# Block one of a two-block transformer: another order of turning, attention and rounding, and the cumulated gates spread by transfer

## The reference

```python
h = _layernorm(x, ln_in_g, ln_in_b)
for layer in range(DEPTH):                      # 2 layers
    proj = jnp.einsum('bsd,de->bse', h, w_in[layer])
    (aq, ak, av, ag, bq, bk, bv, bf, bg, cq, ck, cv, cg) = jnp.split(proj, SPLIT_POINTS, axis=-1)
    # A: 4 heads of differential attention: softmax(q1 k1) - lam * softmax(q2 k2), rotary q and k
    oa = _differential_attention(qa[:, :, 0], qa[:, :, 1], ka[:, :, 0], ka[:, :, 1], va, lam)
    ya = _from_blocks(rms(oa) * subln_g[layer] * (1.0 - lam_init)) * jax.nn.silu(ag)
    # B: 4 heads, softmax(s + cum[q] - cum[k]), cum the cumulated log gates
    logf = jax.nn.log_sigmoid((bf + b_forget[layer]).astype(jnp.float32))
    cum_logf = jnp.cumsum(logf, axis=1).transpose(0, 2, 1)
    ob = _forgetting_attention(_split_heads(bq, HB), _split_heads(bk, HB), _split_heads(bv, HB), cum_logf)
    yb = _from_blocks(ob) * jax.nn.silu(bg)
    # C: 4 heads of stick-breaking attention, z = q k * scale
    #   weights = exp(log_sigmoid(z) + reverse_cumsum(log_sigmoid(-z)) without its own term)
    oc = _stick_breaking_attention(_split_heads(cq, HC), _split_heads(ck, HC), _split_heads(cv, HC))
    yc = _from_blocks(oc) * jax.nn.silu(cg)
    y = jnp.einsum('bse,ed->bsd', jnp.concatenate([ya, yb, yc], axis=-1), w_out[layer])
    h = _layernorm(DEEPNORM_ALPHA * h + y, ln_g[layer], ln_b[layer])
```

## Time and profile before

| | us |
|---|---|
| median of 3 runs | 1867.9 (1865.4 to 1868.3) |
| the profiled execution | 1866.4 |
| its span, first to last instruction | 1864.6 |
| PE busy | 1730.1 |
| block one, by the step list | 0 to about 850 |

### The profile page before, as it was taken

How to read it: one execution, slowest core, us unless ns; L and a number is a source line. 1 busy time by engine, 2 the same in 40 slices (tenths; PEclk the granted TensorE clock), 3 DMA queues, 4 the chain that set the end, 5 groups by cost and what they waited for, 6 DMA issues and landing times. The chain is left out here.

```text
span 1864.6 us, 21015 instructions
## 1 busy us (share of the span) xinstructions
PE 1730.1 (93%) x7750; PEld 1311.8 (70%) x7750; DVE 864.3 (46%) x1487; ACT 799.2 (43%) x1512; POOL 594.1 (32%) x291
## 2 busy tenths in 40 slices
PE   7999999889999998989998999998999899999997
PEld 4766766578667665677564777777787788888786
DVE  5543335553533345454598548475556222221402
ACT  3334446533344455344323555565643334443411
POOL 2613212135313121144120332333265424444440
PEclk9998999899989998999999999999999989999999
DMA  6412222014222120114121222322274333333221
GB/s 177 108 34 68 57 57 68 12 61 112 57 57 57 53 83 23 46 46 130 34 65 51 73 80 68 125 74 68 89 240 135 90 89 93 102 91 102 90 79 45
DMA packets 203832, 148.81 MB, mean 80 GB/s; under 512 B 14926, under 2 KB 183506, under 8 KB 203732
## 3 DMA queue, kind: packets, MB, share of 16 engines
q1 hardware_dynamic: 199056, 132.45, 24.9%
q0 software_dynamic: 4528, 14.95, 2.4%
q10 hardware_dynamic: 148, 0.07, 0.0%
HBM read 136.96 MB, written 10.49 MB: 79 GB/s over the span
## 5 line engine op out<-in xcount | busy, mean ns | idle before, releaser
L1435 POOL TENSOR_TENSOR weights_rounded<-weights_raw,weights_rounded 128x1024 fp32r<-128x1024 f32 (+1 forms) x237 | 566.7, 2406 | 1146.8 <-ACT weights_rounded L1973 1146.7
L1506 PE MATMUL proj<-hT_high,weights_rounded 128*128 128x512 f32 (+1 forms) x1904 | 640.2, 408 | 17.5 <-POOL weights_rounded L1435 7.5
L1506 PEld LDWEIGHTS proj<-hT_high,weights_rounded 128*128 128x128 f32 x1904 | 369.7, 195 | 108.4 <-issue 23.7
L1506 PE MATMUL proj<-hT_low,weights_rounded 128*128 128x512 f32 (+1 forms) x952 | 378.9, 398 | 0.0
L1973 ACT ACTIVATE weights_rounded<-weights_raw 128x1024 fp32r<-128x1024 f32 (+1 forms) x237 | 234.0, 1008 | 112.4 <-DMA weights_raw<-in_w_ffn_down 59.0
L1502 PE MATMUL proj<-weights_rounded,hT_high 128*128 128x512 f32 (+1 forms) x640 | 203.9, 395 | 22.2 <-DVE branches_low L2456 13.5
L1506 PEld LDWEIGHTS proj<-hT_low,weights_rounded 128*128 128x128 f32 x952 | 186.0, 195 | 38.8 <-issue 3.7
L1502 PEld LDWEIGHTS proj<-weights_rounded,hT_high 128*128 128x128 f32 x640 | 122.3, 195 | 50.9 <-issue 15.7
L1629 PE MATMUL score<-qk 64*128 64x256 f32 (+3 forms) x256 | 81.0, 501 | 18.6 <-ACT E L1835 10.2
L1672 PE MATMUL attn_out<-probs_T,V 128*64 128x128 f32 (+1 forms) x560 | 89.2, 294 | 0.0
L1658 PE MATMUL turned_probs<-constants,probs 128*128 128x128 f32 x320 | 61.8, 295 | 18.5 <-ACT probs_T L1863 18.2
(11 more groups left out here) (473 smaller groups left out, 2779.8 us busy)
## 6 DMA issues: line engine op xcount, KB each, us to landing
weights_raw<-in_w_in SPq DMA_DIRECT2D x113, 512.0 KB, 4.0
weights_raw<-in_w_out SPq DMA_DIRECT2D x24, 512.0 KB, 3.8
weights_raw<-in_w_ffn_gate SPq DMA_DIRECT2D x22, 512.0 KB, 3.9
weights_raw<-in_w_ffn_up SPq DMA_DIRECT2D x22, 512.0 KB, 3.8
weights_raw<-in_w_ffn_down SPq DMA_DIRECT2D x22, 512.0 KB, 3.5
gates<-constants POOLq DMA_DIRECT2D x24, 256.0 KB, 3.0
weights_raw<-gates SPq DMA_DIRECT2D x24, 256.0 KB, 3.6
weights_raw<-in_w_in SPq DMA_DIRECT2D x20, 256.0 KB, 3.2
```

What stands on the lines that cost most here:

```text
L1435: nc.gpsimd.tensor_tensor(piece_view(WR, p, "raw"), piece_view(WF, p, "raw"), piece_view(WR, p, "high"), ALU.subtract).then_inc(w_low, 1)
L1506: mm = nc.tensor.matmul(ps[:, on], w_[:, c0:c0 + P], x_[:, k, on], start=first, stop=last)
```

## The change

- **Front.** A tile's turn now stands ahead of the value projection of the tile before it; the norm of the next tile but one stands behind that projection. Weight pieces 4 to 7 are split earlier (`3 * i - 8`).
- **Ticks.** Kind A's rate rises from 1.1 to 1.4, A takes ticks between halves too, and after a job at most one tick is placed where up to three were.
- **C's stages.** `soft2` of an item stands in the same tick as its `soft1`, and `soft3`, `trans` and `pv` one tick earlier than before (lags 1, 2, 3 for 2, 3, 4). `soft3` stands ahead of `soft1` on ACT.
- **Cumulated gates.** `bf` goes ahead of the value projections `bvcv`. The four rows are stored to DRAM behind the second of these (`cum_out`) and read back over all 128 partitions behind the third (`cum_in`), both on POOL's queue; `turn_cum` stays, behind the third. The eight `spread_cum` matmuls and four copies of a layer go.
- **Early rounding.** Chunks 0 to 3 of `y` are rounded into a view over `qk` (`y_early`), so they needn't wait for `hT_high`: 0 and 1 at the gate group of chunk 7, 2 and 3 at that of chunk 4, chunk 4 at that of chunk 5. All five stood at chunk 5's before.
- **The end of a layer.** A tick each stands in or behind the first three parts of `wo`, and two ticks were in the first before.

```diff
-RATES = {"A": 1.1, "B": 2.0, "C": 2.2, "I": 2.0, "M": 1.0, "X": 1.0}
+RATES = {"A": 1.4, "B": 2.0, "C": 2.2, "I": 2.0}
...
-    stages = [("scores", 0), ("soft1", 0), ("soft2", 1), ("soft3", 2), ("trans", 3), ("pv", 4)]
+    stages = [("scores", 0, 0), ("soft3", 2, 1), ("soft1", 0, 0), ("soft2", 1, 0), ("trans", 3, 2), ("pv", 4, 3)]
...
-        while state["fin"] < len(units) and units[state["fin"]]["last"] <= n - DRAIN:
+        while state["fin"] < len(units) and units[state["fin"]]["last"] <= n - (DRAIN - (units[state["fin"]]["kind"] == "C")):
...
-            state["mid"] = between if items[min(state["n"], len(items) - 1)]["kind"] in "BC" else None
+            state["mid"] = between if items[min(state["n"], len(items) - 1)]["kind"] in "ABC" else None
...
-            ticks(3)
+            ticks(1 if items[min(state["n"], len(items) - 1)]["kind"] in "ABC" else 3)
...
     for t in range(NT):
-        value_tiles(0, t)
         if t + 1 < NT:
             turn_rows(t + 1)
-            if t + 2 < NT:
-                steps.append(("ln_in", t + 2))
+        value_tiles(0, t)
+        if t + 2 < NT:
+            steps.append(("ln_in", t + 2))
...
-        def cum_groups(l=l):
-            for h in range(4):
-                group("spread_cum", head=h)
-            group("turn_cum")
-
-        jobs.append((cum_groups, 0.5, 0))
-
+        jobs.append((cum_log, 1, 0))
+
+        def vv_and(t, l=l):
+            vv(t)
+            if t in (1, 2):
+                steps.append((("cum_out", "cum_in")[t - 1], l))
+            if t == 2:
+                group("turn_cum")
...
-            if c == 5:
-                for k in range(5):
-                    steps.append(("split_x", ("y", k, 1)))
+            for k in {7: (0, 1), 4: (2, 3), 5: (4,)}.get(c, ()):
+                steps.append(("split_x", ("y", k, 1)))
...
-            need = 0 if c >= 6 else 4 * (c + 1) + 6 if c < 4 else 16 + 8 * (c - 3) + 6
+            need = 0 if c == 6 else 33 if c == 7 else 4 * (c + 1) + 6 if c < 4 else 16 + 8 * (c - 3) + 6
...
-        state["mid"] = lambda: [tick() for _ in range(2)]
+        state["mid"] = tick
...
-            if t == 1:
-                tick()
+            tick()
...
-            seq = max(p["free_high"], slabs[p["slab"]]["first"] - 3) if i > 3 else -1 if i < 2 else 1
+            seq = max(p["free_high"], 3 * i - 8) if i > 3 else -1 if i < 2 else 1
...
+                if op == "cum_out":
+                    pool.wait_ge(cum_done, arg + 1)
+                    pool.dma_start(cum_rows[arg], cum).then_inc(cum_stored, 16)
+                elif op == "cum_in":
+                    pool.wait_ge(cum_stored, 16 * (arg + 1))
+                    pool.wait_ge(ln_done, NT * (arg + 1))
+                    pool.dma_start(ckb[:, :, :], cum_rows[arg].partition_broadcast(P)).then_inc(cum_spread, 16)
...
-                        for gg in it["cums"]:
-                            wait_group(gg)
+                        dve.wait_ge(cum_spread, 16 * (units[it["unit"]]["layer"] + 1))
+                        wait_group(it["turned_cum"])
```

58 lines of the change are left out of this document (31 added, 27 removed).

## The result

| | before | after |
|---|---|---|
| median, us | 1867.9 (1865.4 to 1868.3) | 1820.4 (1818.8 to 1825.9) |
| the profiled execution | 1866.4 | 1825.9 |
| its span | 1864.6 | 1824.1 |
| PE busy | 1730.1 | 1703.3 |

A forecast was written before the change was run, and what follows sets the result against it. PE was taken to bound the kernel, through its work, waits and half-speed clock. Terms +2.0 - 26 - 10.6 - 2 - 12.6 - 1 = -50.2 from 1866.4 gave 1816.2, stated as 1816.0 us; range 1797 to 1838.

The forecast's parts named there:

- the signs it named for being wrong: Whole kernel: a shorter front, gate-group waits over 10 or under 2 us a layer, or block two moving over 3 us.
- Front, +2.0: Value projections at the start: new turn order costs +6.5 us, earlier weight splits give back 4.5; range +0.5 to +4.5.
- given back: -4.5: Front: the wait for a weight piece, 2.70 us plus 1.8 of half speed behind it, goes through earlier splitting.
- Cumulated gates, -26: Cumulated gates: of 19.1 us a projection and turn, 6.1, remain; -13.0 us a layer, the transfer costing nothing.
- The hole: Cumulated gates, 159.6 to 178.7 us: waits, slow spreading matmuls, turn and half-speed projection, priced at 13.0 us a layer.
- Kind A, -10.6: Kind A's ticks: score waits for exps and half speed fall from 5.1 + 2.2 to 2 us, -5.3 a layer.
- Gate groups, -2: Among gate groups: waits for logits go, ACT's copies come late; 6.5 us waiting and 3.4 clock remain, -1 a layer.
- Early rounding, -12.6: Layer's end, first wo part: waits for chunks 0 and 5 plus half speed fall from 11.7 to 5.4 us, -6.3 a layer.
- Drain, -1: Last attention ticks of a layer: 11.8 us bare against 18.7 with 6.3 of work standing elsewhere, -0.5 a layer.
- the third (the loop of C closing): Rival for kind C: the scores, exp, scan, exp loop closes over one tick for want of buffers, 1928 us; chance 0.03.
- the first (more is hidden): Rival: waits among the gates and for chunk 5 come off short, 24 us more gained, 1792 us; chance 0.15.
- The second: Rival among the gates: ACT and DVE set the pace, scans slow beside weight splits, +18 us, 1834 us; chance 0.20.

## Why the prediction was right, and where its terms were not

The time, 1816.0, is 4.4 us from the median and inside its range, and the sign was right. The terms did worse than their sum, and that they came out together is in good part luck. None of the signs it named for being wrong came: the front is longer, waits among the gates are 7.0 us in either layer, and block two moved by 2.1. By the lengths of the layers in the profiles, 19.3 and 23.3 us went where the terms give 24.1 and 26.1.

- **Front, +2.0.** The front itself was right in every step and a little short in size: +7.9 at the end of the value projections (forecast +6.5, 55.6 to 59.3; its own terms add up to 56.0 to 59.0), and undoing it gives 6.5 back. Right too that the wait for a weight piece goes. What failed is the step "given back: -4.5": it took away 2.70 us of waiting for POOL and left nothing in its place, where 2.38 of waiting for DVE came. The rotations were as slow before, beside a run of eight splits; but kind A's new rate puts the first scores half a projection earlier, and they meet the second rotation before it ends. The prediction asked what else would be late only for the gates, not here. Of the 4.5 some 1.8 us came (26.0 to 24.1 from the value projections to the first scores, one execution each). Undoing the front doesn't undo the splits, so they aren't part of that 6.5.
- **Cumulated gates, -26.** The hole is gone, with nothing in its place and no wait for the transfer: right. As the price of the hole it was sound, as the effect of the edit it was not: alone it gives 15, and the transfer alone undone, with `bf` in its new place, costs 13.4. Order and transfer were not undone together. Two things were left out: that the new place of `bf` closes about half of the hole without any transfer, and that the ticks move with the jobs.
- **Kind A, -10.6.** Its own waits went as told: none for exps in layer one, 1.10 in layer two. But the term was priced where the edit stands. Undone, it costs 48.5, nearly all of it in the last third of the layer (in layer one 9 us among the gate groups and 15 at the end). This is the term that was furthest off, and the one on which the gain rests.
- **Gate groups, -2.** The sum is right: 7.5 + 3.2 became 7.0 + 3.1. The reason given for it is wrong. The prediction spread 6.5 us over the groups as ACT's load; the runs show three waits of 0.5 to 0.9 and one of 4.84, from two turns in a tick. Move that tick and the wait goes while ACT's work and its late scan stay. A size that fits is no evidence for its cause. The lags at which B and C differ stand in the diff, and that B's last item and C's first meet could be read from it.
- **Early rounding, -12.6.** Undone it costs 2.2 us, within the uncertainty of nothing. The single wait of 1.96 for chunk 5 at `wo` came as forecast (2.4), but the half speed that the term charged to the late roundings was not theirs. With the roundings late again the end of layer one (35.2 us, PE busy 26.3, clock 0.90) loses 8.9 + 3.5 us, where the changed kernel loses 7.7 + 7.0.
- **Drain, -1.** Here stands what the rounding was credited with. The end of a layer lost 18.9 us before and loses 14.7 and 14.1 now. The prediction saw "8 ticks bare or nearly so before, now one", then reckoned with the chain of the last item alone and called the rest work that stands elsewhere. That work ran in part at half speed when it stood bare (mean clock of the stretch 0.80). How much of the drain's gain is each edit's isn't shown: A's rate alone makes the end shorter (38.0 us), and no run has C's new stages alone.

So two oversized terms (-26 and -12.6) covered two undersized ones (kind A's rate and the drain). They are not even separate terms: A's rate and the shorter C chain cost 48.5 and 19.2 when undone, together far more than the whole change gives, and A's rate alone gives about 10. The rate spreads the ticks, the shorter chain lets them stand so without waiting, and the order of `bf` takes out the hole between.

Of the rivals, the third (the loop of C closing) did not come, and the first (more is hidden) did not either, since 7.0 of 7.5 us of waiting stay among the gates; but with the doubled turn away only 2.2 are left, as it has it. The second's mechanism was there without its price: a C scan of 128 columns took 2.53 us beside a split and held ACT's exp for 3.10, and with B turned earlier the same collision cost PE next to nothing. The Trainium skill (SBUF — State Buffer, Who interferes with whom) has it that a VectorE instruction with two SBUF inputs and a GpSimd one that reads SBUF exclude each other for a whole instruction. The trace agrees: 0.68 and 0.69 us with POOL idle, 2.07 to 2.77 beside splits of about 2.4 each, and 0.69 in either case for the pass with one input in PSUM.

## What to carry to other kernels

When work is placed by a rate or a credit, ask what is left over at the end of the list: count there the steps with nothing to hide them, for each edit that changes a rate, an order or a job, since that is where the edit pays. Price each edit both alone and undone; where the two differ, the terms share something, and no sum of them is safe even when it comes out right. And where two kinds of items with different lags meet, look at the one step in which both reach the same stage: it needs the same bank twice.

## What the runs showed of the hardware

The same list, with the same waits, doesn't take the same time. Up to the first scores the changed kernel and the one with the spreading matmuls back have one and the same order at the front. From the turn of tile 1 (at 22.31 and 22.23 us) on, PE waits 2.71, 2.71 and 2.38 us in the one and 2.70, 2.70 and 2.38 in the other, and the first scores begin at 82.63 and 79.88. The way there takes 60.3 and 57.7 us with PE busy in 52.5 and 49.9, at a mean clock of 0.94 and 0.97: 2.7 us apart, by how much of it ran at 1.2 GHz. The turn of tile 2 took 1.52 us in the one and 1.07 in the other, and from it to the next turn the mean clock was 0.84 in the one and 1.00 in the other:

```profile
34.19 1.52 PE L1573 MATMUL proj<-constants,h_tok 128*128 128x128 f32 x8 [2.71 <-DVE h_tok L2042]
```
```profile
33.00 1.07 PE L1581 MATMUL proj<-constants,h_tok 128*128 128x128 f32 x8 [2.70 <-DVE h_tok L2052]
```

The same wait of 2.7 us was thus followed by half speed in one execution and not in the other. The four executions of the changed kernel span 7 us. In this kernel an edit worth less than some 4 us is better read from its waits in the trace than from its time.
